# Rows of three activation tensors get other pitches and starts in SBUF

## The reference

```
h = concat(meta_tokens, x)
for i in (0, 1):
    h = layer_norm(ALPHA*h + 0.5*swiglu(h, w_in[i,0], w_out[i,0]))
    h = layer_norm(ALPHA*h + (short_conv if i == 0 else gla)(h))
    h = layer_norm(ALPHA*h + 0.5*swiglu(h, w_in[i,1], w_out[i,1]))
return h[:, 16:]
```

## The kernel before

| tensor | start before | start after | pitch before | pitch after |
|---|---|---|---|---|
| weights_hi, weights_lo | 32896, 65664 | same | 512 a block | same |
| x_hi | 98432 | 98496 | 1152 | 1152 |
| x_lo | 107648 | 107712 | 1280 | 1216 |
| x_hi, x_lo packed (FFN 3) | 98624, 107840 | same | 1024 | 1024 |
| resid and all up to unfolded | 117888 on | 448 lower | - | - |
| mid_hi | 153376 | 152928 | 1088 | 1216 |
| mid_lo | 177312 | 179712 | 1088 | 1216 |
| yc_hi | 159936 | 159488 | 1088 | 1152 |
| yc_lo | 168640 | 168768 | 1088 | 1152 |
| y_hi, y_lo | 153408, 161600 | 256 lower | 1024 | 1024 |
| zg_hi, zg_lo | 207040, 215808 | 256 lower | 1096 | 1096 |

## Time and profile before

### The profile page before, as it was taken

The page is one execution under the profiler, slowest core; times in us unless marked ns, Lnnn a source line. Parts: engine busy times, 40 slices in busy tenths (PEclk is TensorE's granted clock), DMA queues, the critical chain, the costliest instruction groups (busy, mean ns, idle before and its releaser), DMA issues.

```text
span 1017.1 us, 18997 instructions
## 1 busy us (share of the span) xinstructions
PE 1004.7 (99%) x7866; PEld 983.9 (97%) x7866; DVE 723.6 (71%) x1078; ACT 512.4 (50%) x746; POOL 122.2 (12%) x136
## 2 busy tenths in 40 slices
PE   9999999999999999999999999999999999999997
PEld 7999999999999999999999999999989999999885
DVE  5865656689889865557697565667897999766444
ACT  5634344465456543444565434445867766444430
POOL 2000002320002000003220000133152420000000
PEclk9999999999999999999999999999999999999999
DMA  9965656637762966556639665555355738866531
GB/s 255 261 191 171 179 154 179 191 91 211 224 174 82 253 183 175 170 163 179 193 91 256 175 183 155 168 165 160 84 146 145 206 106 247 249 193 201 171 121 41
DMA packets 324263, 176.58 MB, mean 174 GB/s; under 512 B 6658, under 2 KB 320048, under 8 KB 324176
## 3 DMA queue, kind: packets, MB, share of 16 engines
q1 hardware_dynamic: 323664, 174.15, 59.3%
q0 software_dynamic: 480, 1.15, 0.4%
q10 hardware_dynamic: 32, 0.07, 0.0%
HBM read 174.29 MB, written 1.05 MB: 172 GB/s over the span
## 4 chain that ended last, share of the span: by engine, by line
PE 91%; DVE 4%; ACT 1%; issue 1%; POOL 1%; DMA 1%; SPq 0%; POOLq 0%; DVEq 0%; ACTq 0%
PE bank L1311 23%; PE bank L1306 23%; PE bank L1309 23%; PE bank L1325 3%; PE bank L1327 3%; PE bank L1326 3%; PE bank L1469 2%; PE bank L1471 2%; PE bank L1470 2%; PE bank L1350 2%; PE bank L1351 2%; PE bank L1352 2%; DVE weights_lo L821 1%; DMA raw_weights<-in_ffn_w_in_dram 1%; DVE rms L1219 1%
## 5 line engine op out<-in xcount | busy, mean ns | idle before, releaser
L462 ACT ACTIVATE weights_hi<-raw_weights 128x1024 fp32r<-128x1024 f32 x335 | 353.9, 1059 | 410.7 <-PE bank L1311 299.6
L821 DVE TENSOR_TENSOR weights_lo<-raw_weights,weights_hi 128x1024 fp32r<-128x1024 f32 x334 | 415.4, 1250 | 202.9 <-ACT weights_hi L462 201.7
L1306 PE MATMUL bank<-x_hi,weights_hi 128*128 128x272 f32 (+1 forms) x1584 | 226.5, 285 | 0.0
L1311 PE MATMUL bank<-x_lo,weights_hi 128*128 128x272 f32 (+1 forms) x1584 | 225.9, 285 | 0.0
L1309 PE MATMUL bank<-x_hi,weights_lo 128*128 128x272 f32 (+1 forms) x1584 | 223.9, 284 | 0.0
L1306 PEld LDWEIGHTS bank<-x_hi,weights_hi 128*128 128x128 f32 x1584 | 206.3, 188 | 0.6 <-ACT consts L628 0.2
L1311 PEld LDWEIGHTS bank<-x_lo,weights_hi 128*128 128x128 f32 x1584 | 206.9, 188 | 0.0
L1309 PEld LDWEIGHTS bank<-x_hi,weights_lo 128*128 128x128 f32 x1584 | 205.2, 188 | 0.0
L1306 PE MATMUL bank<-mid_hi,weights_hi 128*128 128x272 f32 x462 | 68.2, 288 | 0.0
L1309 PE MATMUL bank<-mid_hi,weights_lo 128*128 128x272 f32 x462 | 68.1, 288 | 0.0
L1311 PE MATMUL bank<-mid_lo,weights_hi 128*128 128x272 f32 x462 | 68.0, 288 | 0.0
(11 more groups left out here) (231 smaller groups left out, 1197.8 us busy)
## 6 DMA issues: line engine op xcount, KB each, us to landing
raw_weights<-in_ffn_w_in_dram SPq DMA_DIRECT2D x176, 512.0 KB, 4.7
raw_weights<-in_ffn_w_out_dram SPq DMA_DIRECT2D x70, 512.0 KB, 4.2
raw_weights<-in_conv_w_in_dram SPq DMA_DIRECT2D x24, 512.0 KB, 4.0
raw_weights<-in_gla_w_in_dram SPq DMA_DIRECT2D x24, 512.0 KB, 3.9
raw_weights<-in_ffn_w_out_dram SPq DMA_DIRECT2D x24, 384.0 KB, 3.5
raw_weights<-in_conv_w_out_dram SPq DMA_DIRECT2D x8, 512.0 KB, 4.9
raw_weights<-in_gla_w_out_dram SPq DMA_DIRECT2D x8, 512.0 KB, 5.0
x_tok<-in_x_dram SPq DMA_DIRECT2D x2, 512.0 KB, 5.3
```

The lines of the kernel that those rows point to most:

```text
L462: nc.scalar.activation(w_hi[:, n % RING, :], raw[:, n % RAW, :], ACT.Copy).then_inc(hi_split, 1)
L821: nc.vector.tensor_tensor(w_lo[:, s, :], raw[:, n % RAW, :], w_hi[:, s, :].bitcast(F32), ALU.subtract).then_inc(lo_split, 1)
L1306: nc.tensor.matmul(ps, block_of(w_hi, n, k - k0), hi[:, k, cols], start=first and k == k0, stop=False)
L1311: mm = nc.tensor.matmul(ps, block_of(w_hi, n, k - k0), lo[:, k, cols], start=False, stop=last and k == k1 - 1)
```

## The change

`x_hi` begins 64 bytes later, behind a pad of 16 words. The area of `x_lo` gets T + 32 words a row instead of T + 48. `mid_hi` and `mid_lo` are declared with T + 32 words a row, of which T are used, with a pad of 8 words between them. `yc_hi` and `yc_lo` get T + 16 words a row and a pad of 16 words between them. The packed x begins 32 words into its areas instead of 48, and the pad before `y_hi` grows from 8 to 56 words. No instruction is added, removed or moved.

```diff
-    CLOSE_AT = 3 * LINE // 4
+    CLOSE_AT = LINE // 2
...
+        pad_x_hi = sb("pad_x_hi", [P, 16])
         x_hi_area = sb("x_hi", [P, KD, T + 16], F32R)
-        x_lo_area = sb("x_lo", [P, KD, T + 48], F32R)
+        x_lo_area = sb("x_lo", [P, KD, T + 32], F32R)
...
-            mid_hi = inner.enter_context(nc.sbuf_tensor("mid_hi", [P, KF, T], F32R))
-            mid_lo = inner.enter_context(nc.sbuf_tensor("mid_lo", [P, KF, T], F32R))
+            mid_hi = inner.enter_context(nc.sbuf_tensor("mid_hi", [P, KF, T + 32], F32R))[:, :, 0:T]
+            inner.enter_context(nc.sbuf_tensor("pad_mid_lo", [P, 8], F32))
+            mid_lo = inner.enter_context(nc.sbuf_tensor("mid_lo", [P, KF, T + 32], F32R))[:, :, 0:T]
...
-            yc_hi = conv.enter_context(nc.sbuf_tensor("yc_hi", [P, KD, T], F32R))
-            yc_lo = conv.enter_context(nc.sbuf_tensor("yc_lo", [P, KD, T], F32R))
+            yc_hi = conv.enter_context(nc.sbuf_tensor("yc_hi", [P, KD, T + 16], F32R))[:, :, 0:T]
+            conv.enter_context(nc.sbuf_tensor("pad_yc_lo", [P, 16], F32))
+            yc_lo = conv.enter_context(nc.sbuf_tensor("yc_lo", [P, KD, T + 16], F32R))[:, :, 0:T]
...
-        pad_y = gb("pad_y", [P, LINE // 8])
+        pad_y = gb("pad_y", [P, 7 * LINE // 8])
```

## The result

The changed kernel takes 1023.15 us (median of 6 runs, 1022.84 to 1023.98) beside 1019.32 us for the kernel before, run beside it (6 runs, 1018.74 to 1021.61). The ratio is 1.0031, 95% interval [1.0019, 1.0044]: slower, where 1014.7 us and faster had been forecast, and just outside the forecast's range. The profiled spans differ by as much: 1021.1 us after, 1017.1 us before.

A forecast was written before the change was run, and what follows sets the result against it. TensorE's matmul pace was taken as the bound; mid -2.4, x_lo -1.8 and yc -0.5 sum to -4.7 us on 1018.8, making 1014.1, or 1014.7 us as median of the runs. The range was 1006.5 to 1022.0 us.

The forecast's parts named there:

- What bounds the kernel: TensorE, busy 99% of the span and held up by nobody: only the pace of its 7866 matmuls can move the time.
- The excess: Matmul start-to-start time above N/2.4 ns, read as the price of the moving operand's place; 10.9 ns for 272-wide x.
- The choice of 256 bytes for the places: Row places counted modulo 256 bytes from the start of a weight block, a modulus chosen and not read from a row.
- x_hi, taken at 0: 2448 matmuls on x_hi, moved to places 64 and 192, forecast at 0; bounds +7.1 and -9.1 us.
- mid, taken at -2.4 us: 1584 matmuls on mid: a gap of 128 bytes between rows saves 1.5 ns each; bounds +1.9 and -8.6 us.
- What had been called "wrong" in advance: Mid's 24 matmuls still at 3.01 us instead of 2.97, meaning a row gap isn't what makes x cheaper than mid.
- x_lo, taken at -1.8 us: 1224 matmuls on x_lo, pitch 1280 to 1216, save 1.5 ns each; bounds +2.0 and -6.1 us.
- the same premise of the gap: 272-wide rows with a gap have excess 10.4 to 11.7 ns, contiguous ones 12.1 to 13.3, so a gap is cheaper.
- The small terms: yc -0.5 us; y and z*gain 0, +-0.8; last projection 0, +-0.8; attention 0, +0.7 to -1.2; packed x unmoved.
- The slower one: Rival: even places, not gaps, made x cheap; x_hi +7.1 us, x_lo +2.0, mid gains nothing, 1028.5 us; chance 0.17.
- no change: Rival: the kernel's time stays the same; chance 0.25, of which 0.20 for gains and losses that cancel.
- the chief case: Within no change's cancelling part (0.20): the last FFN at y's dearer pace, an estimate of +4.0 us.

The follow-up runs named there:

- the shifted weights: Against the first map kernel: weight slots 4160 bytes apart instead of 4096, one row start for a whole FFN; 1032.63 us, one execution.
- The map: Against the kernel before: FFN input tiles from the fourth on read rows from a cleared area at chosen places and pitches; 1026.33 us, one execution.
- the version with all operands by the map: Against the kernel before: x_hi, x_lo, mid_hi and yc at pitch 1280, place 192, mid_lo at pitch 1152; 1012.11 us, ratio 0.9932.

## Why the prediction was wrong

**What bounds the kernel** was read rightly: no wait changed, and all of the +4.0 us is pace of TensorE. The excess was counted from N/2.4 ns, which these products reach in no profile at the full clock; where the trace of mid and yc alone records a granted clock of 0.555 it is borne out: on average, without the few distances over 500 ns, 204.2 ns a matmul of 272 columns, 192.6 of 256 and 384.8 of 512, which times 0.555 are 113.4, 106.9 and 213.6 ns. The choice of 256 bytes for the places, and of the weight block as the point from which they are counted, had been an assumption; the shifted weights bear it out.

**The step that failed is x_hi, taken at 0.** It rested on the attention's 256-wide tiles, which stood at places 64 and 192 with an excess of 10.8. Measured were +4.5 us on these 2448 matmuls, within the bounds of +7.1 and -9.1. The row had the right place and pitch but not the right width. The map shows that the order turns round with the width: at pitch 1152 places 64 and 192 are the cheap ones for 256 columns (2800 against 2840 to 2858) and the dear ones for 272 (3013 against 2960). The attention itself went the other way, 2.82 to 2.85 us, when x_hi moved.

**mid, taken at -2.4 us, brought +0.1.** The excess of 12.1 was put down to rows without a gap. By the map a gap of 0 and one of 128 bytes cost the same at mid's old places, 3000. The prediction also had mid visit odd places before and after; mid_lo went to even ones, and its matmuls became 0.4 us dearer while those of mid_hi became 0.3 us cheaper. The experiment on mid alone gave +0.07 us. What did make mid cheaper is mid_hi at a pitch at which every row has the place 192: 3.01 to 2.96 us, -2.6 us for its 1386 plain matmuls, in the version with all operands by the map. What had been called "wrong" in advance, mid still at 3.01, is what came.

**x_lo, taken at -1.8 us, brought +0.5**, on the same premise of the gap; moved by itself it cost 1.3 us in its own runs and 3.2 us in those of x_hi. That one operand's rows set the pace of another's was no term of the sum at all. The prediction had seen that a place can have two paces (y in the earlier trace rows) but priced it for what only moves, not for x.

**The small terms** were right in kind: yc -0.2 us for -0.5, y -0.5 us and the last projection -0.3 within their +-0.8, the last FFN 0, the attention +0.25 within its bounds, z*gain 0. Together they take back 0.8 us. y's share is one of its two paces rather than a price of the change: with the same addresses it brought nothing in the second run of mid and yc alone.

**The rivals.** The slower one, that the even places were the good ones and not the gaps, had the right sign and the right operand, x_hi: +4.5 of its +7.1 us, x_lo +0.5 of +2.0, mid +0.1 where it said 0. Its time of 1028.5 us was 5 us too high, since x did not get as dear as yc's 126.7 ns. "Even" is also not the rule: place 192 at pitch 1280 is even and the best, 128 the worst. The chance of 0.25 for no change was mostly (0.20) for gains and losses that cancel; the chief case, an estimate of +4.0 us for the last FFN at y's dearer pace, did not come: it kept 2.72 us. The rest of it was for a price of 0 for every place. The runs do not agree with that: kernels that differ in nothing but addresses took 1012.11 to 1028.79 us.

**What stays open.** Which of its two paces an arrangement takes is not settled. 0 and 128 at pitch 1152 ran in 2960 and in 3000, y at 113.3 and 117.1 ns from the same place, and the reason why x_lo's new rows hold x_hi's at the dear pace is only located, not explained. What in the chip makes a distance dear is not shown by any run: they tell where the price lies, not what makes it. z*gain at another pitch was not tried.

## What to carry to other kernels

Where a matmul's start-to-start distance stands above its columns divided by 2.4 a ns (113.3 ns for 272 columns, where x took 124.2 and yc 126.7 here), compare it between stages, and look at where the moving rows lie relative to the stationary blocks, modulo 256 bytes, before looking for a wait. Take a price only from a row of the same width, pitch and place, since the order of places turned round between 256 columns (2800 ns a unit at 64 and 192, 2840 and 2858 at 128 and 0) and 272 (3013 against 2960), and change all rows of a unit together: here x at a pitch of 1280, which gives each row the same place, took 3.0 us off the span at place 192 and added 8.5 at place 128, and with mid_hi and yc at 192 too the span fell by 6.4 us. Moving a tensor ahead of the weights or between weights and rows can then be an edit with a price of its own: the weights' start, moved by 64 bytes alone, cost 5.0 us in the last FFN here and took 3.7 us off x in the other three.

## What the hardware showed that was not expected

- The pace of a matmul depended on the distance of its moving row from its weights: 123.3 to 126.7 ns at 272 columns, 113.3 to 120.0 at 256, in rows of matmuls without a wait, and steady for whole stages: the last FFN has the same 2.72 us a unit in the kernel before, the changed one and every other profiled at the full clock, but for the one with moved weights and the two with replaced tiles.
- The same arrangement ran at either of two paces (2960 and 3000 ns a unit; 2720 and 2827 for the packed rows of the last FFN in the real tiles and in the map). That what ran ahead of it decides is an assumption.
- The executions of one kernel lie in two groups some 3 us apart (the kernel before: 1018.3 to 1019.9 and 1021.4 to 1023.1 us). The profile of the second run of mid and yc shows where such a gap can come from. First its start, with the first matmul on x:

```profile
8.91 1.06 PE L1455 MATMUL bank<-idle 128*128 128x512 bf16 x2
...
12.96 0.57 PE L1446 MATMUL bank<-x_hi,weights_hi 128*128 128x272 f32 x1
13.33 0.43 PE L1447 MATMUL bank<-x_lo,weights_hi 128*128 128x272 f32 x1
13.56 0.43 PE L1446 MATMUL bank<-x_hi,weights_hi 128*128 128x272 f32 x1
```

and the first matmuls of the same kinds in the kernel before:

```profile
7.75 0.59 PE L1452 MATMUL bank<-idle 128*128 128x512 bf16 x2
...
10.22 0.37 PE L1443 MATMUL bank<-x_hi,weights_hi 128*128 128x272 f32 x1
```

Two matmuls of 512 columns take 1.06 us instead of 0.59, the second 426 ns after the first instead of 216, and those of 272 columns follow one another by 227 ns (13.33 to 16.51 us), 1.2 columns a ns, instead of by 125. So TensorE runs at about half its pace there: 2.7 us are lost by the first matmul on x and 4.4 us by the first unit of plain ones (18.12 us instead of 13.73). A window of the profile over this stretch prints a granted clock of 1.00 in both kernels, but that is how it prints a stretch without a record: in the trace the record of the full clock begins at 5.75 us in the kernel before and at 17.59 us here. In both, eight matmuls of 512 columns had gone ahead by 5.75 us, so the same work got the full clock in one execution and not in the other. That the upper group is this in the other kernels too is likely, but they have no profile of it.
- Two executions ran at a lower granted clock, with no other time of their kernels near theirs. The one with a profile, of mid and yc alone, took 1654.72 us; its page grants about half the clock in every slice (0.555 in the trace's record from 5.92 us on, 0.56 in the windows), and the other nine executions of this kernel took 1018.1 to 1022.5 us:

```profile
PEclk6555555555555555555555555555555555555555
```

The other, of x at place 160, took 1409.42 us at a mean granted clock of 0.655. Why the clock stayed down in these two is not shown.
